# Up products of three feed-forward layers by one level of Strassen's algorithm

## What is computed

```
D_MODEL, SEQ, D_FF = 1024, 512, 2816

def rmsnorm_2(x, g):
    y = xf * lax.rsqrt(jnp.mean(xf * xf, axis=-1, keepdims=True) + EPS)
    return y * g

def swiglu(h, wg, wu, wd):
    return (jax.nn.silu(h @ wg) * (h @ wu)) @ wd

for i in range(2):
    x = x + 0.5 * swiglu(rmsnorm_2(x, ffn_norm1[i]), ffn1_wg[i], ffn1_wu[i], ffn1_wd[i])
    ...  # sliding-window attention (i = 0), latent attention (i = 1)
    x = x + 0.5 * swiglu(rmsnorm_2(x, ffn_norm2[i]), ffn2_wg[i], ffn2_wu[i], ffn2_wd[i])
```

## Time and profile before

| | |
|---|---|
| median of 3 runs | 2659.52 us (2659.14 to 2660.36) |
| span of the profiled execution | 2659.0 us, 30833 instructions |
| PE busy | 2630.2 us (99%), 12546 matmuls |
| PEld busy | 2197.8 us (83%) |
| DVE busy | 1437.9 us (54%) |
| ACT busy | 987.7 us (37%) |
| POOL busy | 320.2 us (12%) |
| HBM | 258.91 MB moved by DMA, mean 97 GB/s |

### The profile page before, as it was taken

The page is one execution under the profiler, slowest core; times in us unless marked ns, Lnnn a source line. Parts: engine busy times, 40 slices in busy tenths (PEclk is TensorE's granted clock), DMA queues, the critical chain, the costliest instruction groups (busy, mean ns, idle before and its releaser), DMA issues.

```text
span 2659.0 us, 30833 instructions
## 1 busy us (share of the span) xinstructions
PE 2630.2 (99%) x12546; PEld 2197.8 (83%) x12560; DVE 1437.9 (54%) x2266; ACT 987.7 (37%) x1626; POOL 320.2 (12%) x388
## 2 busy tenths in 40 slices
PE   9999999999999999999999999999999989999999
PEld 8888888888887788889988888888888788888887
DVE  7637547574757444356774343453434676543433
ACT  4334334242454222246642222422223586432221
POOL 0000010000021000015530000100000586200000
PEclk9999999999999999999999999999999999999999
DMA  5332225423232444453323222232222101232222
GB/s 161 121 101 80 95 79 190 154 85 106 80 101 90 107 103 107 98 109 104 104 96 110 95 95 88 88 111 95 95 95 83 61 19 42 88 109 95 95 91 68
DMA packets 276389, 258.91 MB, mean 97 GB/s; under 512 B 40324, under 2 KB 266647, under 8 KB 276247
## 3 DMA queue, kind: packets, MB, share of 16 engines
q1 hardware_dynamic: 276231, 256.93, 31.6%
q10 hardware_dynamic: 16, 0.00, 0.0%
HBM read 242.23 MB, written 14.68 MB: 97 GB/s over the span
## 4 chain that ended last, share of the span: by engine, by line
PE 90%; DVE 3%; ACT 3%; issue 2%; POOL 2%; DMA 0%; SPq 0%; POOLq 0%; DVEq 0%; ACTq 0%
PE bank L1186 29%; PE bank L1188 29%; PE bank L1187 29%; PE bank L1353 1%; DVE Wl L1928 1%; ACT Wh L1565 0%; PE bank L1417 0%; POOL Wl L2495 0%; ACT Z L1851 0%; POOL TMP L2502 0%; DVE Pl L2450 0%; PE bank L1285 0%; PE bank L1513 0%; ACT Hh L1841 0%; PE bank L1197 0%
## 5 line engine op out<-in xcount | busy, mean ns | idle before, releaser
L1186 PE MATMUL bank<-Hh,Wl 128*128 128x512 f32 x2136 | 838.9, 393 | 0.8 <-DVE Hl L1947 0.8
L1188 PE MATMUL bank<-Hh,Wh 128*128 128x512 f32 x2136 | 832.3, 390 | 0.0
L1187 PE MATMUL bank<-Hl,Wh 128*128 128x512 f32 x2136 | 831.8, 389 | 0.0
L1928 DVE TENSOR_TENSOR Wl<-RAW,Wh 128x1024 fp32r<-128x1024 f32 (+2 forms) x420 | 493.7, 1219 | 171.2 <-ACT Wh L1565 170.4
L1565 ACT ACTIVATE Wh<-RAW 128x1024 fp32r<-128x1024 f32 (+2 forms) x454 | 441.2, 1022 | 382.8 <-PE bank L1188 358.4
L1186 PEld LDWEIGHTS bank<-Hh,Wl 128*128 128x128 f32 x2136 | 401.4, 188 | 86.8 <-issue 1.7
L1187 PEld LDWEIGHTS bank<-Hl,Wh 128*128 128x128 f32 x2136 | 401.5, 188 | 84.0 <-issue 1.7
L1188 PEld LDWEIGHTS bank<-Hh,Wh 128*128 128x128 f32 x2136 | 401.2, 188 | 83.9
L1186 PE MATMUL bank<-Ph,Wl 128*128 128x512 f32 x1152 | 451.9, 392 | 0.8 <-DVE Wl L1928 0.5
L1188 PE MATMUL bank<-Ph,Wh 128*128 128x512 f32 x1152 | 448.6, 389 | 0.0
L1187 PE MATMUL bank<-Pl,Wh 128*128 128x512 f32 x1152 | 448.2, 389 | 0.0
(11 more groups left out here) (336 smaller groups left out, 2427.4 us busy)
## 6 DMA issues: line engine op xcount, KB each, us to landing
RAW<-in_ffn_wg SPq DMA_DIRECT2D x44, 1024.0 KB, 5.2
RAW<-in_ffn_wu SPq DMA_DIRECT2D x44, 1024.0 KB, 5.2
RAW<-in_ffn_wd SPq DMA_DIRECT2D x32, 1024.0 KB, 4.8
RAW<-in_w_up SPq DMA_DIRECT2D x22, 1024.0 KB, 5.1
RAW<-in_w_in SPq DMA_DIRECT2D x20, 1024.0 KB, 5.1
RAW<-in_ffn_wd SPq DMA_DIRECT2D x16, 768.0 KB, 4.3
bias_scratch<-M SPq DMA_DIRECT2D x16, 512.0 KB, 8.0
RAW<-in_w_down SPq DMA_DIRECT2D x8, 1024.0 KB, 4.8
```

The source lines that it names most:

```text
L1186: mm(o, ll, rh, start=start, stop=False)
L1187: mm(o, lh, rl, start=False, stop=False)
L1188: return mm(o, lh, rh, start=False, stop=stop)
L1928: tt(Wl[:, n % 3, x:y], RAW[:, n % 2, x:y], f(Wh[:, n % 3, x:y]), ALU.subtract).then_inc(*w_lo.up(*([("w_lo", n)] if i else [])))
```

## The change

In the layers s1, s2 and s3 each up product is done by one level of Strassen's algorithm in Winograd's form. A tile of weights is cut in 2 by 2 blocks: its 8 chunks of input features in even and odd ones, its 256 columns in two halves. The input is cut the same way: even and odd chunks, and the first and last 256 tokens. Seven products of blocks take the place of eight. Every product is 4 chunks x 3 matmuls of 256 columns, 84 of them a tile where there were 48 of 512 columns.

- **Weights.** POOL forms four sums of 512 columns a tile from RAW (`w_sum`): two into NS (part of M), two in place in RAW. ACT and DVE then split four pieces a tile (`w_fill`: three of 1024 columns, one of 512), 3584 columns where there were 2048. Wh and Wl hold two tiles' three pieces; the fourth piece alternates between WS and a part of Hh and Hl.
- **Inputs.** For each pair of chunks, ACT writes the scaled input (`hc_raw`), four sums of 256 columns are made (`t_sums`, on POOL for the first three pairs, on DVE for the last), and ACT and DVE split 1792 columns (`hc`).
- **Results.** The products gather in three regions of PSUM a tile. ACT copies a region of 256 columns three times at steps between products (`cp`), and DVE adds to a copy or multiplies by the norm's factor (`c11`, `c22`, `c12`, `c21`, each 256 columns with one input in PSUM). The rest of the multiplication by the norm's factor is POOL's (`rm`, 256 columns for the right half of features, 512 for the left). `silu_f`, `glu_f` and the pair follow as before, `glu_f` now with both inputs in SBUF.
- **Order.** `period(n, prev)` is the steady pattern: products 1, 2, 6, 5 and 7 of tile n between products 4 and 3 of the tile before, with the sums and splits of tile n + 1 (`feed`). So the preparation runs one tile ahead. After the first pair of tiles of the next third come the down tiles of the last one (after its "a" tile), as before otherwise. The first tile of a layer is prepared in the last down tile (or the end of the attention) before it.

The diff, cut to the parts that the prediction speaks of:

```diff
...
+FAST = ("s1", "s2", "s3")
+MIRROR = ("s3",)
+FIRST_PLACE = 2
+PRODUCTS = {1: (0, 0, 0, "fx"), 2: (0, 1, 1, "fz"), 3: (3, 0, 2, "fy"), 4: (2, 1, 6, "fx"), 5: (1, 0, 3, "fy"),
+            6: (1, 1, 5, "fx"), 7: (2, 0, 4, "fx")}
+PIECE_DONE = {0: (1, 2), 1: (5, 6), 2: (7, 4), 3: (3,)}
...
+    def feed_tile(n):
+
+        def end():
+            do("w_fill", n, 3)
+            assert now["split"] == n
+            now["split"] += 1
+            load()
+
+        def plain():
+            assert now["split"] == n
+            split()
+            load()
+
+        if n < NW and is_up(tiles[n]):
+            now["feed"] += [lambda: do("w_sum", n)] + [lambda p=p: do("w_fill", n, p) for p in range(3)] + [end]
+        elif n < NW:
+            now["feed"].append(plain)
...
+    def hc_chunk(tag, c, gname, base):
+        do("hc_raw", tag, c, xv[c], gname, base)
+        if c % 2:
+            do("hc_sum", tag, c // 2)
+            do("hc", tag, c // 2, 0)
+            do("hc", tag, c // 2, 1)
...
+        def prod(n, i, r0=0, r1=4):
+            ring = {1: xs, 2: banks, 5: ys}.get(i)
+            if ring and r0 == 0:
+                ring.take((PRODUCTS[i][3], n))
+            do("prod", n, i, r0, r1, tag)
...
+        def post(n, m):
+            h, j, x = place[n]
+            if x == "a":
+                do("silu_f", n, m)
+                return
+            na = place[h, j, "a"]
+            t = ("t_f", na, m)
+            do("glu_f", na, n, m)
+            pair_p(2 * j + m, "tmp", t, ("glu", t))
+
+        def scaled(n, m):
+            do("rm", n, m, norm)
+
+        def period(n, prev):
+            feed_tile(n + 1)
+            prod(n, 1)
+            prod(n, 2)
+            feed(2)
+            cp(n, 1)
+            prod(prev, 4)
+            do("c11", n)
+            feed()
+            prod(n, 6)
+            do("c21", prev, norm)
+            feed()
+            cp(n, 2)
+            prod(prev, 3)
+            scaled(prev, 1)
+            post(prev, 1)
+            prod(n, 5)
+            do("c12", prev)
+            scaled(prev, 0)
+            feed(5)
+            prod(n, 7)
+            cp(n, 3)
+            do("c22", n)
+            post(prev, 0)
+            extra(2)
...
+    norm_begin("s1", "RF", (0, 1))
+    ffn_fast("s1", "s2", "ffn_norm1_2", 8)
+    norm_begin("s2", "RF", (0, 1))
+    ffn_fast("s2", "b", "mix_norm_2", 8)
...
+    def t_sums(eng, tt, out_, tag, r):
+
+        eng.wait_ge(*at(("hc_raw", tag, 2 * r + 1)))
+        tt(hb(r, 3, 4), hb(r, 7, 8), hb(r, 0, 1), ALU.subtract).then_inc(*out_.up(("hc_sum", tag, r, 0)))
+        tt(hb(r, 4, 5), hb(r, 2, 3), hb(r, 7, 8), ALU.subtract).then_inc(*out_.up())
+        eng.wait_ge(*at(("hc_sum", tag, r, 0)))
+        tt(hb(r, 5, 6), hb(r, 2, 3), hb(r, 3, 4), ALU.subtract).then_inc(*out_.up(("hc_t2", tag, r)))
+        eng.wait_ge(*at(("hc_t2", tag, r)))
+        tt(hb(r, 6, 7), hb(r, 1, 2), hb(r, 5, 6), ALU.subtract).then_inc(*out_.up(("hc_sum", tag, r, 1)))
...
+            elif kind == "prod":
+                n, i, r0, r1, tag = s
+                piece, part, x, region = PRODUCTS[i]
+                name = (region, n)
+                begins = i in (1, 2, 5)
+                o = (vacant(name) if begins and r0 == 0 else bank(name))[:, 0:256]
+                pe.wait_ge(*at(("w_lo", n, piece)))
+                if i == 6 or i == 7 or i == 4:
+                    pe.wait_ge(*at(("cp", n, {6: 1, 7: 2, 4: 3}[i])))
+                elif i == 3:
+                    pe.wait_ge(*at(("c22", n)))
+                wh, wl = (w[:, 512 * part:512 * part + 512] for w in up_piece(n, piece))
+                for r in range(r0, r1):
+                    pe.wait_ge(*at(("hc_lo", tag, r, int(x > 3))))
+                    xh, xl = (w[:, 256 * x:256 * x + 256] for w in hc_at(tag, r))
+                    rr = slice(128 * r, 128 * r + 128)
+                    mm(o, wl[:, rr], xh, start=begins and r == 0, stop=False, skip_group_check=True)
+                    mm(o, wh[:, rr], xl, start=False, stop=False, skip_group_check=True)
+                    ins = mm(o, wh[:, rr], xh, start=False, stop=r == 3, skip_group_check=True)
+                if r1 == 4:
+                    ins.then_inc(*bank_full.up(("prod", n, i)))
...
+            elif kind == "w_fill":
+                n, piece = s
+                act.wait_ge(*at(("sum", n, piece) if piece else ("raw", n)))
+                for event in released(n, piece):
+                    act.wait_ge(*at(event))
+                if piece == 3:
+                    act.wait_ge(*at(("h_read", tiles[n][0][:-1])))
+                    all_gone(("hc_ok", tiles[n][0][:-1]))
+                run(shaped(up_piece(n, piece)[0], piece), up_source(n, piece), ACT.Copy).then_inc(
+                    *w_hi.up(("w_hi", n, piece)))
...
+            elif kind == "w_fill":
+                n, piece = s
+                wh, wl = up_piece(n, piece)
+                dve.wait_ge(*at(("w_hi", n, piece)))
+                tt(shaped(wl, piece), up_source(n, piece), f(shaped(wh, piece)), ALU.subtract).then_inc(
+                    *w_lo.up(("w_lo", n, piece), *([("w_lo", n)] if piece == 3 else [])))
...
+            elif kind == "c12":
+                n, = s
+                t = tmp(("t_f", n, 0))[:, 256:512]
+                dve.wait_ge(*at(("cp", n, 2)))
+                dve.wait_ge(*at(("prod", n, 3)))
+                tt(t, bank(("fy", n))[:, 0:256], t, ALU.add).then_inc(*dve_out.up(("c12", n), free=("fy", n)))
...
+            elif kind == "glu_f":
+                na, nb, m = s
+                ta, tb = tmp(("t_f", na, m)), tmp(("t_f", nb, m))
+                dve.wait_ge(*at(("silu_f", na, m)))
+                dve.wait_ge(*at(("rm", nb, m)))
+                dve.wait_ge(*at(("c21", nb)))
+                tt(ta, ta, tb, ALU.mult).then_inc(*dve_out.up(("glu", ("t_f", na, m)), free=("t_f", nb, m)))
...
+            elif kind == "w_sum":
+                n, = s
+                v = raw_blocks(n)
+                a11, a12, a21, a22 = v[:, :, 0, 0, :], v[:, :, 1, 0, :], v[:, :, 0, 1, :], v[:, :, 1, 1, :]
+                n1, n2 = (NS[:, z:z + 512].rearrange("p (r m) -> p r m", r=4) for z in (0, 512))
+                pool.wait_ge(*at(("raw", n)))
+                for event in gone(("hc_ok", tiles[n][0][:-1])):
+                    pool.wait_ge(*event)
+                if up_before(n) is not None:
+                    pool.wait_ge(*at(("w_lo", up_before(n), 1)))
+                tt(n1, a21, a22, ALU.add).then_inc(*w_sum.up(("sum", n, 0)))
+                pool.wait_ge(*at(("sum", n, 0)))
+                tt(n2, n1, a11, ALU.subtract).then_inc(*w_sum.up(("sum", n, 1)))
+                tt(a21, a11, a21, ALU.subtract).then_inc(*w_sum.up(("sum", n, 2)))
+                pool.wait_ge(*at(("sum", n, 1)))
+                pool.wait_ge(*at(("w_lo", n, 0)))
+                tt(a12, a12, n2, ALU.subtract).then_inc(*w_sum.up(("sum", n, 3)))
...
+            elif kind == "rm":
+                n, m, nv = s
+                t, z = tmp(("t_f", n, m)), 256 * m
+                pool.wait_ge(*at(("c22", n) if m else ("c12", n)))
+                pool.wait_ge(*at(("R", nv)))
+                tt(t[:, z:512], t[:, z:512], RVIEW[norm_R[nv]][:, z:512], ALU.mult).then_inc(*pool_out.up(("rm", n, m)))
...
```

More of the change, by code:

```diff
@@ L196, in weight_tiles, with is_up, places @@
     return tiles
+def is_up(tile):
+    return tile[0][:-1] in FAST and tile[0][-1] in "ab"
+def places(tiles):
+    col, held, holder, ring, i = [], [], [None] * 14, FIRST_PLACE, 0
+    for n, (name, key, _) in enumerate(tiles):
+        tag = name[:-1]
+        i = i + 1 if n and tiles[n - 1][0][:-1] == tag else 0
+        side = (i + (tag in MIRROR)) % 2
+        if tag not in FAST:
+            pieces = [(2048 * ring, 2048)]
+            ring = (ring + 1) % 3
+        elif is_up(tiles[n]):
+            pieces = [(3072 * (i % 2) + 1024 * x, 1024) for x in range(3)]
+        elif key[0] == 2:
+            pieces = [(1536 * key[1], 1536)]
+        else:
+            pieces = [(3072 * (i % 2), 2048)]
+        if tag in FAST:
+            ring = 0
+            if tag in MIRROR:
+                pieces = [(6144 - c - w, w) for c, w in pieces]
+        col.append([c for c, _ in pieces])
+        slots = [range(c // 512, (c + w) // 512) for c, w in pieces]
+        if is_up(tiles[n]):
+            slots.append(range(12 + side, 13 + side))
+        held.append([[x for j, x in enumerate(holder[s] for s in rng) if x and x not in [holder[s] for s in rng][:j]]
+                     for rng in slots])
+        for piece, rng in enumerate(slots):
+            for s in rng:
+                holder[s] = (n, piece)
+    return col, held
 def order(tiles):
     steps, home, before = [], {}, {}
-    banks, tmps = Ring(range(8), home, before), Ring(range(3), home, before)
+    banks, tmps, diags = Ring(range(8), home, before), Ring(range(3), home, before), Ring((7,), home, before)
     NW = len(tiles)
```

(31 more changed lines are left out.)

316 lines of the change are left out of this document (284 added, 32 removed).

## The result

| | |
|---|---|
| before, same chip | 2659.52 us (2659.14 to 2660.36) |
| after | 2811.28 us (2810.68 to 2813.57) |
| ratio | 1.0571, 95% interval 1.0556 to 1.0586 |
| span of the profiled execution | 2809.6 us, 150.6 more than before |

The account below looks back on a forecast made before the run. The prediction took PE as the bound before, the port shared by DVE and POOL after. From 2659.5 us: steady periods +82.6, periods at PE's pace -12.0, layer starts +18, together +88.6, giving 2748 us, range 2640 to 2815.

Parts of the forecast that it names:

- the port shared by DVE and POOL: DVE instructions with two SBUF inputs take turns with POOL's: 11.5 to 14.1 us a period, chance 0.74.
- the rows named beforehand: Signs: POOL's sums near 1.8 us, DVE's 1024-column splits 1.5 to 2.3, PE near 80% busy, waits before products 6 and 7.
- the slight overlap that rows 7 and 8 showed: DVE and POOL instructions overlap a little at the port, so 11.5 us a tile was used, not 13.0.
- the steady term: 51 periods in the layers' steady pattern at 12.5 us instead of 10.88: +82.6 us.
- The +0.95 for the wait for `c12`: POOL's 512-column factor step stands waiting for DVE's `c12` in periods after a b tile: +0.95 us per tile.
- Turns at 11.5: Low bound of a tile's POOL time with port turns back to back: 7.44 + 3 x 0.94 + 3 x 0.41 us.
- 12 to 13 throughout: Sign in the steady pattern: 12 to 13 us from tile to tile.
- PE's saving: 84 matmuls at 0.120 us make 10.08 us a tile, 0.80 less; over 66 tiles PE alone gives 53 us back.
- The formula that the prediction set beside it: Warm matmul gap of N/2.4 + 2.5 ns: 9.17 us a tile, PE alone giving 79 us; the rows were preferred.
- Rival 3, the clock: The lock plus PE's clock falling in long gaps, a fifth of 51 periods: +55 us, 2803 us; chance 0.03.
- Layer starts: The input's last pair passes copies, chained sums and splits before the norm: 6 us a layer, between 2 and 10, +18.
- its worst case: Top of the lock's range: 51 x 3.22 us for periods and 30 for layer starts, 2842 us, stopped at 2815.

Follow-up runs that it names:

- Experiment 1: The changed kernel with the second input of six DVE instructions a tile read from a PSUM bank of ones, layer starts untouched: 2701.4 us.
- experiment 6: The changed kernel with a tile's last post step (`glu_f` and pair, or silu) moved behind the next tile's first copy and `c11`: 2772.4 us.
- experiment 2: The changed kernel with `c12` directly behind product 3, ahead of the pair and `glu_f` of the other half: 2807.5 us.
- experiments 4 and 5: The changed kernel with 20 spare matmuls before product 6, where the tile before is a b tile (2811.9 us) or the tile in work is (2816.4 us).
- Experiments 9 to 11: On experiment 6: input sums cut to 16 columns, 2752.0 us; first two tiles' weight sums cut to 32, 2752.9; input sums all on DVE, 2752.5.

## Why the prediction was right, and where it was off

- **Slower, by the port shared by DVE and POOL: shown.** Experiment 1 takes the meeting away and 110 us go. Of the rows named beforehand, DVE's splits of 1024 columns have medians of 1.97 and 1.98 us, and gaps stand in front of product 6, ended by ACT's copies. POOL's four sums have means of 1.49 to 1.79 us, but medians of 1.29, 1.59, 1.73 and 1.30, so not all near 1.8: where POOL's sum runs at full speed it is DVE's split that is long (1.28 us at 1833.80 beside 2.25 at 1833.91). PE is busy 86% of the seven tiles above, not 80%. The Trainium skill (SBUF — State Buffer, Terms) speaks of a lock held for the full instruction. With nothing overlapping the durations make 13.0 us a tile; four distances in a row took 12.0 to 12.1 in the mean in experiment 6, so the slight overlap that rows 7 and 8 showed is there, and the measurement decides.
- **The size of the steady term: right, in part by luck.** 51 x 12.5 forecast 51 x 2.42 = 123 us above PE's 10.08; measured 125, of which 109 go with the meeting (experiment 1). But its make-up was not as forecast. The +0.95 for the wait for `c12` isn't there (experiment 2: 4 us); ACT's order, a copy behind the pair, took 39 us (experiment 6). Turns at 11.5 were not reached: spread over the same 51 periods, the 86 us that experiment 6 leaves above 10.08 make 11.8, and the stretches between the down tiles 12.0 to 12.1. The rotary table in s1 was not thought of. The distances are not 12 to 13 throughout but 10.1 and 12 to 17 by turns, since PE first uses up what is prepared.
- **PE's saving: right**, 66 x 0.80 = 53 us; the undisturbed distance is 10.08 (experiment 1), as from the earlier trace rows. The formula that the prediction set beside it is given by the Trainium skill (TensorE: Matmul & The Clock Gate, Back-to-back issue gap) for an isolated matmul; its 9.17 us a tile was not reached.
- **Rival 3, the clock: the fall came true, its price is not shown.** It was argued away with PE busy 46.66 of 50 us in short pieces. The gaps came as one piece of 2 to 4 us per two tiles, and behind nearly each of them the granted clock was 0.50 for 2 to 4 us. The slower matmuls add up to some 41 us, those at the starts included; experiments 4 and 5 took 24 and 26 us of that away and won nothing.
- **Layer starts: the term that failed.** "I estimate 6 us a layer, between 2 and 10: +18." By subtraction from the spans, 151 + 53 - 125 = 79 us lie outside the 60 distances, of which PE's gaps at the starts are 24.3 (s1), 17.8 (s2) and 20.8 (s3), 62.8 together; 8 are slower matmuls in the start sections, and the rest is not taken apart. These 61 us over the estimate are nearly the whole distance between 2748 and 2811, and that the range still held the time is owed to its width: its worst case had 30 us for the starts. The error was to price only the chain of the *last* input pair, and to count the three others as hidden beside PE's down tiles. They are not: DVE's next `add_x` stands behind the low parts of the pair, these wait for POOL's sums, and POOL is behind eight weight sums of the first two tiles. Experiments 9 to 11 show 20 us for each kind of sum; how the remainder divides between the chain itself and the port stays open, as experiment 1 leaves the starts as they were. The trace of before held a part of what was needed: DVE already took 1.71 us a chunk in that place, 3.4 a pair, before any chained sum was put into it.
